# Cutting the 640 tokens of every projection at 128 instead of at 320

## What is computed

```python
def mixer(u, p, ctx):
    proj = u @ p['w_in']                                   # 1024 -> 6672 columns
    hy_in, s_z, s_xbc, s_dt, a_q, a_k, a_v, g = jnp.split(proj, SPLIT_IDX, axis=-1)
    hy_y = hyena_branch(hy_in, p)                          # long convolution by DFT
    ssm_y, ssm_state = ssm_branch(s_z, s_xbc, s_dt, p, h0) # Mamba-2 scan
    att = latent_attention(...) or ctx_attention(...)
    gate = jax.nn.sigmoid(g).reshape(B, L, N_BRANCH, D_MODEL)
    merged = (gate[:, :, 0] * (hy_y @ p['hy_proj'])
              + gate[:, :, 1] * (ssm_y @ p['ssm_proj'])
              + gate[:, :, 2] * (att @ p['attn_proj']))
    return merged @ p['w_out'], side

def ffn(h, p):                                             # 1024 -> 2816 -> 1024
    return (jax.nn.silu(h @ p['ffn_w_gate']) * (h @ p['ffn_w_up'])) @ p['ffn_w_down']
```

## Time and profile before

| what | value |
|---|---|
| device time, two runs | 3044.25 and 3047.03 us, median 3045.64 |
| profiled execution, first to last instruction | 3042.1 us |
| TensorE matmul busy | 2797.4 us, 92% |
| TensorE weight load busy | 2333.0 us, 77% |
| VectorE busy | 1274.1 us, 42% |
| ScalarE busy | 793.7 us, 26% |
| GpSimd busy | 347.7 us, 11% |
| mean granted TensorE clock | 0.958 |

### The profile page before, as it was taken

One profiled execution on the slowest core, in us unless ns is written; L12 is line 12 of the kernel. 1 busy time (PEld: TensorE's weight loads), 2 busy tenths in 40 slices (PEclk: granted clock), 3 DMA queues, 4 the chain that ended last, 5 costly groups with the idle time before them and its releaser, 6 DMA issues. The chain is left out here.

```text
span 3042.1 us, 38189 instructions
## 1 busy us (share of the span) xinstructions
PE 2797.4 (92%) x16461; PEld 2333.0 (77%) x16461; DVE 1274.1 (42%) x1799; ACT 793.7 (26%) x1084; POOL 347.7 (11%) x214
## 2 busy tenths in 40 slices
PE   6989987989999699999889899879999997999996
PEld 2846543769999499999839465446799986999996
DVE  5475475372322522222254745564623324312224
ACT  3222111252222522212242221112512235222121
POOL 1021124000112200000110202230001131000001
PEclk9989998999999899999989899989999998999998
DMA  7120102212222222222061100021122222222211
GB/s 256 43 76 14 42 14 56 68 55 70 77 69 84 89 78 70 84 70 69 30 228 31 61 28 28 28 64 64 57 70 83 71 84 83 73 81 70 84 59 45
DMA packets 207684, 213.42 MB, mean 70 GB/s; under 512 B 29064, under 2 KB 192208, under 8 KB 207126
## 3 DMA queue, kind: packets, MB, share of 16 engines
q1 hardware_dynamic: 207510, 210.92, 21.4%
HBM read 207.49 MB, written 3.41 MB: 69 GB/s over the span
## 5 line engine op out<-in xcount | busy, mean ns | idle before, releaser
L654 PE MATMUL ps<-arena_parts,weights_parts 128*128 128x320 f32 x9824 | 1648.2, 311 | 25.8 <-DVE normed_parts L726 24.0
L654 PEld LDWEIGHTS ps<-arena_parts,weights_parts 128*128 128x128 f32 x9824 | 1495.9, 188 | 36.7 <-DVE normed_parts L726 27.0
L606 DVE TENSOR_TENSOR weights_parts<-weights,weights_parts 128x2048 fp32r<-128x2048 f32 (+2 forms) x142 | 301.5, 2123 | 805.7 <-ACT weights_parts L598 805.7
L654 PE MATMUL ps<-normed_parts,weights_parts 128*128 128x320 f32 x2368 | 541.6, 310 | 0.0
L654 PEld LDWEIGHTS ps<-normed_parts,weights_parts 128*128 128x128 f32 x2368 | 397.9, 189 | 0.0
L598 ACT CAST weights_parts<-weights 128x2048 fp32r<-128x2048 f32 (+2 forms) x142 | 242.7, 1711 | 181.4 <-PE ps L654 181.4
L679 POOL TENSOR_TENSOR normed<-normed 128x640 f32<-128x640 f32 x56 | 92.8, 1658 | 1105.1 <-ACT normed L1921 946.7
L640 PE MATMUL ps<-normed,weights 128*128 128x320 f32 x768 | 211.9, 434 | 0.7 <-DVE arena L1453 0.7
L640 PEld LDWEIGHTS ps<-normed,weights 128*128 128x128 f32 x768 | 144.5, 190 | 70.3 <-issue 12.7
L1984 POOL TENSOR_TENSOR arena<-arena 128x640 f32<-128x640 f32 x32 | 54.3, 1698 | 776.1 <-DVE arena L1622 776.1
L1657 DVE TENSOR_TENSOR arena<-arena,ps 128x640 f32<-128x640 f32 x44 | 36.1, 821 | 187.6 <-PE ps L654 187.6
(11 more groups left out here) (253 smaller groups left out, 2365.5 us busy)
## 6 DMA issues: line engine op xcount, KB each, us to landing
weights<-in_w_in_dram SPq DMA_DIRECT2D x48, 1024.0 KB, 5.0
weights<-in_ada_w_dram SPq DMA_DIRECT2D x28, 1024.0 KB, 5.2
weights<-in_ffn_w_gate_dram SPq DMA_DIRECT2D x22, 1024.0 KB, 5.1
weights<-in_ffn_w_up_dram SPq DMA_DIRECT2D x22, 1024.0 KB, 5.2
weights<-in_ada_w_dram SPq DMA_DIRECT2D x10, 2048.0 KB, 12.4
weights<-in_ffn_w_down_dram SPq DMA_DIRECT2D x16, 1024.0 KB, 5.1
weights<-in_w_out_dram SPq DMA_DIRECT2D x8, 1024.0 KB, 5.1
weights<-in_ffn_w_down_dram SPq DMA_DIRECT2D x8, 768.0 KB, 4.4
```

What stands on the lines that cost most here:

```text
L606: Vc(dve.tensor_tensor(part_view(m, 1), raw_view(n), part_view(m, 0).bitcast(F32), ALU.subtract) .then_inc(vector_done, 1), "part", m)
L654: m = pe.matmul(tokens(s)[0:cols, lo:hi], a[:, k, oc], x[k][:, lo:hi], start=k == 0 and i == 0, stop=k == n - 1 and i == 2)
```

## The change

The cut of the 640 tokens moves from 320 to 128: the first matmul of each pair takes the context tokens, the second the latent tokens. `tokens(s)` moves with it, so that the cut still falls between the two banks: the result lies in columns 384 to 1024 of the slot instead of 192 to 832. `dense`, `dense_parts`, `channel_sum` and `hidden` all take their parts from `HALVES`; every reader takes its columns from `tokens`.

```diff
         def tokens(s):
 
-            return ps[:, 1024 * s + 512 - T // 2:1024 * s + 512 + T // 2]
+            return ps[:, 1024 * s + 512 - LP:1024 * s + 512 + LS]
...
-    HALVES = ((0, T // 2), (T // 2, T))
+    HALVES = ((0, LP), (LP, T))
```

## The result

The changed kernel takes 3344.16 us (3341.69 to 3346.63, two runs) against 3045.64: 1.098 times the time before, with a 95% interval of 1.096 to 1.100. The forecast was 3336, within 3270 to 3440.

The account below looks back on a forecast made before the run. TensorE was taken to bound the kernel, in line 654. A 110 ns load plus a 231 ns long matmul made 48 ns more a pair, +290 us over 6048 pairs; span 3332 plus 3.5 gave 3336 us, range 3270 to 3440.

Parts of the forecast that it names:

- What bounds the kernel: TensorE, busy 2797 of 3042 us, mostly in line 654's three-product projections: 1805.6 us, 59% of the span.
- The load, 110 ns, read from line 854: Line 654's 128-column weight loads follow 110 ns apart, as line 854's plain 32-bit loads do; a short matmul covers only 59 to 67.
- The long matmul, 231 ns: Line 654's 512-column matmul takes 231 ns, the middle between 226.7 and 234.6.
- the 13.3 ns: Line 654's 320-column matmul spacing of 146.6 ns less 133.3 at 2.4 GHz; a fixed part or by columns, left undecided.
- The pair's 341 ns: Line 654's short and long matmul together: 110 + 231 = 341 ns against 293.2, +48 ns for 6048 pairs.
- One load ahead, not two: Only one weight load can run ahead of its matmul; a pair of 300 to 330 ns would indicate a second.
- The plain projections, -2 to 0 us: Line 640's plain 32-bit pairs: 538 ns against 544, so -2 to 0 us over 384 pairs.
- The first tiles behind a norm and the lower clock: Two cancelling terms in line 654: up to 5 us hidden in waits for VectorE, up to 4 us more at 1.2 GHz.
- The readers at no cost: ScalarE and VectorE read the same 640 columns 192 columns further up in PSUM, 692 ns at either place: no cost.
- the load hides: Rival in line 654: the load keeps its port only 63 ns, a pair stays at 293 ns, 3046 us; chance 0.09.
- the plain rate for narrow matmuls: Rival in line 654: 128 columns cost two plain instructions of 109 ns, a pair 449 ns, 3989 us; chance 0.06.
- the clock, which was to fall: Rival: lower array use costs TensorE the full clock in a tenth of the pairs, +206 us, 3542 us; chance 0.04.

Follow-up runs that it names:

- 3168 pairs in one place: Only the feed-forward part cut at 128 and 512, in the kernel before the change: 3200.8 us, 1.0509 times before, 48.9 ns a pair.
- the runs with 96 and 64 columns: Changed kernel with weight loads of the second and third product cut to 96 or 64 output channels in 3752 pairs: 3253.8 and 3154.1 us.
- the three shorts together: Changed kernel with each channel tile's three short matmuls first, then its three long ones: 3343.0 us.
- the three-part kernel: Changed kernel with the 512 columns of the three-product line taken as two matmuls of 256, each with its load: 3388.2 us.

## Why the prediction was right

*What bounds the kernel.* TensorE, in line 654, with 1.8 us of waits for its weights. Right: 299.5 us more in that line gave 302.7 us more in the span, and 3168 pairs in one place cost as much each as all 6048.

*The load, 110 ns, read from line 854.* Right within 2 ns: the loads' start times give 108.4. That a load of this type keeps its port as the plain one of the same width does had been inferred from durations alone; the start times and the runs with 96 and 64 columns show it, the slope included.

*The long matmul, 231 ns.* The size was off here, not the mechanism. The middle of 226.7 and 234.6 was a compromise between two accounts of the 13.3 ns. The account by columns is the true one: the start times give 234.5. This is the term that was mis-sized, by 3.5 ns, and the load's 1.6 ns too much happened to make good about half of it. The pair's 341 ns were 1.5 short of 342.5, and 1.5 x 6048 = 9 us is about the 8 us by which the forecast missed.

*One load ahead, not two.* Supported by the three shorts together, by the pair of 342.5 ns, where 300 to 330 had been named as the sign of a second load ahead, and by the loads' starts: two begin 108 ns apart, and then none until the long matmul's 234.5 ns are over, though the second of the two needs the port for no more than its own 108.

*The plain projections, -2 to 0 us.* Line 640 is busy for 212.9 us; in the profile of before it was 211.9, so +1.0. A trifle, but of the other sign. By the start times inside a run of these instructions, four of 320 columns take 4 x 269 = 1076 ns, and in the changed kernel two of 128 and two of 512 take 109 + 112 + 432 + 429 = 1082. The 272 and 428 ns that the sum used were averages over whole timeline rows, too coarse for a difference of 6 ns.

*The first tiles behind a norm and the lower clock*, taken to cancel: the waits for line 726's tiles fell from 24.0 to 22.6 us, an absorption of 1.4 us where up to 5 were allowed. What line 654 takes beyond its full-clock spacings went from 18 to some 20 us (2105.0 less 6048 x 0.3425 and less 14 for the block with 16 weight columns), where up to 4 more were allowed. So they do nearly cancel.

*The readers at no cost.* VectorE 1274.1 and 1276.1 us, ScalarE 793.7 and 793.8: right within 0.2%.

*The rivals.* That the load hides is refuted by the result; the plain rate for narrow matmuls by the same and by the block with 16 weight columns; the clock, which was to fall, is 0.962 for 0.958 before. The Trainium skill, "TensorE: Matmul & The Clock Gate", section on LDWEIGHTS, charges a load its columns at 1.2 GHz, 107 ns for 128, 80 for 96, 53 for 64 (estimates by its formula); the traces say 108, 82 and at most 58. So the rule holds within 2 ns for the two that can be read; the transposes' 63 ns stay outside it. The same page's "Back-to-back issue gap" gives 81 and 131 ns for 128 and 512 columns in a stream of loads and matmuls, 212 ns a pair; here it is 342.5.

## What to carry to other kernels

Where every matmul brings its own weight load, a matmul must be as wide as its neighbour's load is long, here 240 to 256 moving columns for 128 weight columns in the rounded 32-bit type; two parts of 320 cost nothing, 256 and 384 nothing on average, 128 and 512 cost 10% of the kernel. "Busy" won't tell, since a matmul that waits for its weights counts as busy: read the spacing (stretch divided by count) and whether the load row has idle time. To price a cut that a trace lacks, look for a line whose matmuls are narrower than their loads, and take the spacing there; check by the loads' duration that they are of the same kind, for the transposes' would have misled (63 ns for 128 columns).

## What the runs showed of the hardware that I had not expected

A matmul in the rounded 32-bit type takes 0.455 to 0.458 ns a moving column at the full clock, 10% over the 0.417 of 2.4 GHz, and by columns, not by instruction: 290 to 295 ns for 640 columns in two parts whether these are 320 and 320, 256 and 384, or, with narrow loads, 128 and 512. Plain 32-bit products take twice the clock's rate and little more, by start times 429 ns for 512 columns and 269 for 320, against 426.7 and 266.7. At the lower clock level (86.5 to 91.5 us of the trace before, granted clock 0.50) the start times of line 654 are 266.7 ns apart, which is 320 columns at 1.2 GHz and nothing over, so what holds the rounded type back doesn't show there. What it is stays open.

Where load and cover are nearly equal, a few ns are lost beyond the longer of the two: 2.5 ns a pair at the cut at 224, 1.1 at 240, 7.2 ns a load in the three-part kernel, but none on average at 256. Why is open as well.
